# Three products of a recurrence's side work issued ahead of TensorE's wait for an inverse

## The reference, cut to what matters

```
def wkv7(r, w, k, v, a, b):
    def step(state, inp):
        r_t, w_t, k_t, v_t, a_t, b_t = inp
        sa = jnp.einsum('bhij,bhj->bhi', state, a_t)
        state = (state * w_t[:, :, None, :] + sa[..., None] * b_t[:, :, None, :]
                 + v_t[..., None] * k_t[:, :, None, :])
        return state, jnp.einsum('bhij,bhj->bhi', state, r_t)
...
gates = jax.nn.sigmoid(p[..., OFF_G:]).reshape(bsz, seq, N_BRANCH, D_MODEL)
merged = (gates[:, :, 0] * y_a + gates[:, :, 1] * y_b
          + gates[:, :, 2] * y_c + gates[:, :, 3] * y_d)
x = x + gt1 * (merged @ w_o[l])
```

## Time and profile before

| | us |
|---|---|
| median of three runs | 2311.21 |
| lowest and highest | 2310.29, 2315.83 |
| the profiled execution, its own time | 2317.72 |
| its span in the profile | 2315.7 |

### The profile page before, as it was taken

How to read it: one execution, slowest core, us unless ns; L and a number is a source line. 1 busy time by engine, 2 the same in 40 slices (tenths; PEclk the granted TensorE clock), 3 DMA queues, 4 the chain that set the end, 5 groups by cost and what they waited for, 6 DMA issues and landing times.

```text
span 2315.7 us, 27377 instructions
## 1 busy us (share of the span) xinstructions
PE 2147.8 (93%) x10790; PEld 1703.9 (74%) x10790; DVE 1296.3 (56%) x1824; ACT 456.1 (20%) x839; POOL 846.9 (37%) x1009
## 2 busy tenths in 40 slices
PE   6889798998799999989989999999899989999996
PEld 5668586676588888866767878787766668878784
DVE  6775655436763243674444745637636747727274
ACT  2112301210100000313342211113133432102011
POOL 1323233232244444432214444444432224444442
PEclk7999899997799999999999999999999989999998
DMA  8867577576799999985528989898965449899885
GB/s 280 221 141 167 114 151 145 121 181 161 229 236 196 196 192 193 192 174 115 108 57 194 194 184 195 179 200 187 197 136 101 92 102 186 178 198 191 184 193 141
DMA packets 121783, 393.60 MB, mean 170 GB/s; under 512 B 25220, under 2 KB 27396, under 8 KB 121272
## 3 DMA queue, kind: packets, MB, share of 16 engines
q0 software_dynamic: 96624, 350.46, 71.3%
q1 hardware_dynamic: 25032, 41.39, 5.6%
HBM read 387.92 MB, written 3.92 MB: 169 GB/s over the span
## 4 chain that ended last, share of the span: by engine, by line
PE 74%; DVE 14%; DMA 7%; issue 2%; ACT 1%; POOL 1%; SPq 0%; DVEq 0%; ACTq 0%; POOLq 0%
PE ps L1582 62%; DMA w_lo<-in_w 4%; PE ps L1710 2%; DMA arena<-in_ada 2%; PE ps L1611 2%; PE ps L1739 2%; PE ps L1725 1%; DVE work L668 1%; PE ps L1896 1%; DVE g_lo L462 1%; POOL w_lo L429 1%; DVE arena L556 1%; DVE arena L669 1%; DMA w_hi<-in_w 1%; DVE small L855 1%
## 5 line engine op out<-in xcount | busy, mean ns | idle before, releaser
L1582 PE MATMUL ps<-h_hi,w_hi 128*128 128x512 f32 x1760 | 711.1, 404 | 27.1 <-DVE h_lo L512 13.3
L1582 PE MATMUL ps<-h_hi,w_lo 128*128 128x512 f32 x1760 | 690.1, 392 | 0.0
L1582 PE MATMUL ps<-h_lo,w_hi 128*128 128x512 f32 x1760 | 690.0, 392 | 0.0
L424 POOL DMA_DIRECT2D w_hi<-in_w x334 | 187.4, 561 | 1289.9 <-PE ps L1582 1203.3
L1582 PEld LDWEIGHTS ps<-h_hi,w_hi 128*128 128x128 f32 x1760 | 332.6, 189 | 126.2 <-issue 29.9
L1582 PEld LDWEIGHTS ps<-h_hi,w_lo 128*128 128x128 f32 x1760 | 332.8, 189 | 71.3
L1582 PEld LDWEIGHTS ps<-h_lo,w_hi 128*128 128x128 f32 x1760 | 333.4, 189 | 64.8 <-issue 2.2
L429 POOL TENSOR_SCALAR w_lo<-w_hi 128x1024 fp32r<-128x1024 f32 x334 | 359.5, 1076 | 45.3 <-DMA w_hi<-in_w 39.8
L1582 PE MATMUL ps<-g_hi,w_hi 128*128 128x512 f32 (+1 forms) x792 | 313.8, 396 | 28.6 <-DMA w_lo<-in_w 19.5
L432 POOL DMA_DIRECT2D w_lo<-in_w x334 | 301.0, 901 | 106.0 <-POOL w_lo L429 106.0
L1582 PE MATMUL ps<-g_lo,w_hi 128*128 128x512 f32 (+1 forms) x792 | 307.1, 388 | 0.0
(11 more groups left out here) (373 smaller groups left out, 2080.1 us busy)
## 6 DMA issues: line engine op xcount, KB each, us to landing
w_hi<-in_w POOLq DMA_DIRECT2D x334, 512.0 KB, 4.0
w_lo<-in_w POOLq DMA_DIRECT2D x334, 512.0 KB, 5.8
arena<-in_ada SPq DMA_DIRECT2D x40, 512.0 KB, 9.4
x<-in_ada SPq DMA_DIRECT2D x8, 512.0 KB, 7.9
x<-in_xT SPq DMA_DIRECT2D x1, 2048.0 KB, 10.0
x<-in_xT SPq DMA_DIRECT2D x4, 512.0 KB, 4.4
arena<-in_memT SPq DMA_DIRECT2D x2, 1024.0 KB, 7.1
out_y<-arena SPq DMA_DIRECT2D x4, 512.0 KB, 2.6
```

Source lines behind the costliest of these rows:

```text
L424: pool.dma_start(w_hi[:, q % SLOTS, :], A["w"][q]).then_inc(S(f"high_in{q % SLOTS}"), 16)
L1582: mm = pe.matmul(bank, w[:, slot, cols], a(k), start=(k == 0 and i == 0), stop=(k == blocks - 1 and i == 2))
```

## The change

In front of TensorE's three waits for the recurrence's inputs, the first three steps of the side work are now issued. Nothing else is changed: VectorE's and ScalarE's orders stay as they are, and so does the order of the DMAs on SyncE and GpSimd.

```
             steps = beside()
+            for _ in range(3):
+                next(steps)
             pe.wait_ge(S("tT_in"), 16 * 8)
             pe.wait_ge(S("bd_used"), 18)
             pe.wait_ge(S("s5_y"), 2)
```

## The result

| | before | changed |
|---|---|---|
| median, us | 2314.93 (6 runs) | 2324.95 (6 runs) |
| lowest, highest, us | 2310.29, 2318.43 | 2319.33, 2342.14 |
| profiled execution, its span | 2315.7 | 2320.7 |

The ratio to the kernel before is 1.0048, with a 95% interval of 1.0029 to 1.0067: about 11 us slower, 7 to 16. A later second measurement of the changed kernel gave the same ratio, 1.0048 (1.0030 to 1.0066). The three runs of the kernel before that the prediction started from (median 2311.21) lay low; with more runs its median is 2315 to 2316.

What follows compares the result with a forecast made beforehand. TensorE's own sequence was taken to bound the kernel. The terms -4.1 - 2.8 + 11.9 + 1.0 - 1.6 summed to +4.4 us, giving 2315.5 us from the 2311.2 median; range 2306 to 2323, the forecast's own 2313 to 2322.

Steps and rivals of the forecast that it cites:

- What bounds the kernel: Around the inverse's wait and loop: TensorE's own sequence sets the end, so changes of some us in it are passed on.
- Term 1: TensorE's wait for the inverse: 18 moved matmuls fill the gap and are missing behind the loop, -4.1 us.
- Term 2: Loop's first chunk: with about 1.8 us of gap left the clock stays full, -2.8 us.
- Term 3: In the loop: ten tiles wait for VectorE or ScalarE to read their banks in their own slot, +11.9 us.
- Term 4: At the wait: an earlier GpSimd weight load delays the inverse's landing, +1.0 us, bounds 0 and 2.0.
- Term 5: Behind the loop: the late weight piece should now be in time, -1.6 us, bounds -1.6 and 0.
- rival (b): Between moved steps and first chunk: weight load delays the inverse until the clock falls, +8.2 us, 2319.4 us; chance 0.22.
- Rival (c): In the loop's bank-wait clusters: the clock falls; one +7, all four +15.7 us, 2326.9 us; chance 0.10.
- Rival (a): In the loop: the waits for banks cost nothing and only the gain is left, -7.5 us, 2303.7 us; chance 0.10.

Runs made afterwards that it cites:

- fifth experiment: Changed kernel with VectorE's and ScalarE's side work moved three places forward and GpSimd's weight load held until the inverse has landed; 2307.67 us, ratio 0.9967.
- sixth experiment: As the fifth experiment, with four steps in front of the wait and both readers four places forward instead of three; 2306.78 us, ratio 0.9961.
- first: Changed kernel with two steps in front of the wait instead of three; 2313.84 us, ratio 0.9998.
- third: Changed kernel with VectorE's and ScalarE's side work also moved three places forward; 2314.36 us, ratio 0.9991.
- seventh: Changed kernel with ScalarE's side work alone moved one place forward; 2318.82 us, ratio 1.0023.
- eighth: Changed kernel with VectorE's side work alone moved one place forward; 2318.43 us, ratio 1.0008.
- fourth experiment: Kernel before, no step moved, with only one GpSimd weight load issued about as early as in the change; 2316.17 us, ratio 1.0007.
- second: Changed kernel with GpSimd's weight load held until the inverse has landed; 2325.91 us, ratio 1.0045.

## Why the prediction was wrong, step by step

The direction of the sum and its main term held; the time, 2324.95 us, lies above the range of 2306 to 2323, and the chance of 0.61 for no measurable change was on the wrong case.

- **What bounds the kernel: right.** Over the first five experiments the sum of TensorE's three distances changed by -8.6 to +6.2 us, and the timed differences went the same way, from -8 to +10, though a single profile's sum and the timed difference lay up to 4 us apart.
- **Term 1, the moved steps, -4.1 us: right.** The 18 matmuls stand in the gap, and C is shorter by 4.1 us for them.
- **Term 2, the clock, -2.8 us: this failed.** It rested on 1.8 us of idle time being left and on the full clock being kept through them. There were 4.6 and 4.3 us. The clock fell in both profiles, and over B 0.9 us was gained in the first and none in the second, whose half clock came later and reached past the first bank wait. With 1.4 us left (fifth experiment) the clock held, and B is 3.0 us shorter than before, so the price was right. The condition was not met, and it was itself too weak: in the sixth experiment's profile 1.9 us were left and the clock fell. The row at 318 us, by which I had judged a gap under 2 us to be safe, did not carry over to this place.
- **Term 3, the bank waits, +11.9 us: right**, 11.6 in both profiles, in the ten places named. The first and third experiments remove all ten, the seventh and eighth four and six.
- **Term 4, the late inverse, +1.0 us: mis-sized.** It measured 2.8 and 2.6, above my upper bound of 2.0. That bound came from a spread of landing times under a different mix of loads, and no row showed a whole new 512 KB load laid over the reads. The fourth experiment shows that the early load delays the reads. Over seven profiles with it Read is 2.8 us above the 7.91 on the mean; with it held it was 7.90, 7.89, 9.13 and 8.55, so holding it brings back most of the old landing, with some spread left. Which of the two loads does it was not separated. By the rule of the Trainium skill, "DMA: Bandwidth & Descriptors", section "Queues, rings and completion order", I had said that the sum would lean to its upper bound, and kept 1.0 in it all the same; the runs agree with the direction of the rule, and the size went past the bound.
- **Term 5, -1.6 us:** -1.2 in one profile and not to be seen in the other.

With measured terms the first profile adds up: A +2.9, B +10.6 (11.56 less 0.92 from the clock), C -5.2, together +8.3; the second +2.5, +11.6, -3.7, together +10.4. The timed ratio gives 7 to 16 us, so both lie inside it. The +8.3 is 3.9 above the +4.4 of the sum: 1.9 of that is term 2, 1.9 term 4 (in A), 0.4 term 5, less the 0.3 by which term 3 came out under its 11.9. What happened is the prediction's rival (b), for which I had worked out +8.2 us and given 0.22: the load delays the inverse until the clock falls all the same. I had written that it would come in from a delay near 1 us, and then taken exactly that delay as likeliest while counting on the full clock. That was the step that failed. Rival (c) came in part, in the second and eighth experiments, for one cluster each; I had TensorE idle for about a third of such a stretch, and it was 1.1 to 1.3 of 3 us; by the rule of the Trainium skill ("TensorE: Matmul & The Clock Gate", section "A second HAM failure mode: psum-queue depth-cycling") the clock would fall at every cluster, and no profile here shows that. Rival (a) is refuted.

The start was also off: 2311.2 us was the median of three runs, and with more it is 2315 to 2316. Of the 9.5 us between 2315.5 and 2324.95 about 4 are this. With the same sum on 2314.93 the forecast would have been 2319.3 and the upper end of the range near 2327, so that the time lies outside the range is owed in part to the start, while terms 2 and 4 were wrong whatever the start.

What stays open is why the reads of the inverse land 1.2 us late in one profile and 5.1 in another under the same early load, and 1.2 and 0.6 late with the load held. Part of it lies in the issue: SyncE needed 5.27 and 5.10 us to issue the eight reads in these two held profiles and 5.36 and 4.98 in the two latest early ones, where it needed 4.4 to 4.5 in all the others. What stretched the issue is not shown.

## What to carry to other kernels

When one engine's hand-written order is moved forward, lay it against its partners' orders and count, for each buffer it takes, how many places stand between the reader and the taker: with two steps none of the tiles met its own slot's reader, with three ten did, at 1.2 us each. Move the readers by as many places; here that turned +11 us into about -2, and with the weight load held as well into -8. And ask what the moved work releases, because the first matmul of a piece also starts a weight load, and that load landed on the transfer that the moved work was meant to wait for.

## What the runs showed of the hardware that I had not expected

A 512 KB load on GpSimd's queue, issued 2.3 to 2.8 us behind the first of SyncE's eight 32 KB reads, with a second one 1.9 us behind it, went with a use of the inverse 1.2 to 5.1 us later than the 7.9 us from issue to use of the kernel before. With both held it took 7.9 us twice, 8.6 and 9.1, so not all of this need be theirs. An idle time of 1.4 or 1.5 us on TensorE in front of the loop left the clock full (fifth and second experiment), and one of 1.9 us was followed by 3.4 us at 1.2 GHz (sixth). And TensorE's clock fell in the middle of a loop whose matmuls had 1.7 to 1.9 of 3 us busy (second and eighth experiment), while the cluster at the same slots in both profiles of the changed kernel kept it: the same waits do not always cost the same.
